# Attention on one NeuronCore: the value projection with its operands swapped, and the logits' scale, bias and row extreme in one VectorE instruction per block

## The chip, the cores and the metric

The kernel runs on one NeuronCore of a Trainium2 chip. The metric is the device time of one execution in microseconds (us); the time of a kernel is the median of its runs. Engines: PE is TensorE, DVE is VectorE, ACT is ScalarE, POOL is GpSimd, SP issues the weight transfers.

## What is computed

256 tokens of width 1024 go through three layers in float32. Layer A has a convolution and pooling mixer, layers B and C an attention mixer; each mixer is followed by a feed-forward block with a causal convolution, and layer C also by a gate of a side input. The two attention mixers are what the change touches:

```
q, k, v = split(rmsnorm(h) @ w_in)            # 16 heads of 64 each (layer C: 4 of the values are 128 wide)
# layer B: 8 "moba" heads (causal softmax with a table bias), 8 "fox" heads (forgetting bias)
p = softmax(q @ k.T * 64**-0.5 + bias, causal);  y = p @ v
# layer C: 4 "diff" heads: y = (softmax(q1 k1 + b1) - lam * softmax(q2 k2 + b2)) @ v, then an RMS norm
#          8 "stick" heads: stick-breaking weights from log_sigmoid and a suffix sum, y = w @ v
h = h + y @ w_out
```

## The kernel before

**Projections.** Activations lie with channels on partitions and tokens along the free dimension. Every float32 weight block is split into a rounded high part `wh` (ACT, line 480) and the rest `wl` (DVE, line 785, or POOL, line 434). A unit (`unit`) is 24 matmuls: 8 blocks of 128 input channels, three products each (lines 1243 to 1245), weights stationary, 256 tokens moving. Weights stream through a ring of four slots; the split of unit u+4 begins when unit u is done. A norm's factor `rstd` is applied after the projection: the reader of the bank multiplies by `rstd`.

**Attention.** `attention` exists once for each engine. The work is in 8 pairs of heads, 3 units each: q is unit 3n, k is 3n+1, v is 3n+2. Layer 0 of `attention` (layer B of the model) has four moba and four fox pairs, layer 1 four diff and four stick pairs. The order on each engine is written out by hand in a loop over j. For pair n, PE runs `scores(n)` (lines 1354 and 1356 for moba, fox and diff), and after two or three units `turn(n)`: it transposes the values (line 1377) and the softmax's result (line 1392), and `weigh(n)` multiplies the two (lines 1415 and 1417). Between `scores` and `turn` stand DVE's `logits(n)` (scale and bias: lines 1038 and 1040; row maxima: lines 1043 and 1045), ACT's `softmax_exp(n)` (line 641: four exponentials with their sums) and DVE's `normalise(n)` (lines 1059 and 1065). DVE's `read_out(u)` (line 1019) copies each unit of q, k or v out of its bank, times `rstd`. ACT's `copy_turned` takes the transposes out of PSUM: line 657 the probabilities, line 659 the values.

**Banks.** The units use three banks in turn, unit 3 of each layer a fourth. A unit waits on the semaphore `bank_read` until the unit three before it has been read. The first two units of an attention stage are begun by `begin`, behind the last unit of a down projection, whose two banks are read by `residual_down` (line 950, two counts of `bank_read` for each chunk).

Of the kernel before, what the change touches and what calls it, by code (L numbers as in the profile page):

```python
# [75 lines left out]
def build_program(nc, streams, x_in, p_in, vectors_in, pool_in, gate_in, rel_in, onehot_in, count_in, out):  # L76
# [55 lines left out]
    with ExitStack() as ctx:  # L132
# [37 lines left out]
        lam = sb("lam", [P, 8])  # L170
        eps = sb("eps", [P, 1])
# [50 lines left out]

        stick_values = psum[:, 5, SEQ:2 * SEQ].rearrange("p (b d) -> p b d", b=2)
# [3 lines left out]
        EARLY = QKV_BANKS  # L227

        def qkv_bank(u):
            return turned_banks[:, 0, 0:SEQ] if u == EARLY else psum[:, u % QKV_BANKS, 0:SEQ]  # L230

# [69 lines left out]
        turned_read = sem("turned_read")  # L301
        relu_done = sem("relu_done")
# [170 lines left out]
        def _(act):  # L473
# [149 lines left out]
            def attention(layer, name, out_name):  # L623
# [10 lines left out]
                def softmax_exp(n):  # L634
# [3 lines left out]
                    for half in range(2):  # L638
                        for b, (a, z) in enumerate(((0, P), (P, SPAN))):
                            at = 2 * b + half  # L640
                            last = nc.scalar.activation(e[:, half, a:z], e[:, half, a:z], ACT.Exp,  # L641
# [4 lines left out]
                def copy_turned(n):  # L646
# [8 lines left out]
                    else:  # L655
                        m = 1 if order[n][0] == "diff" else 2
                        nc.scalar.activation(probs_t[n % 2][:, 0:m, :], turned_banks[:, 0:m, 0:SPAN], ACT.Copy)
# [33 lines left out]
                for j in range(PAIRS + 2):  # L691
# [9 lines left out]
                    if j < PAIRS:  # L701
                        round_next(3 * j)
                    if late:
                        log1p(j - 1)
# [73 lines left out]
        def _(dve):  # L778
# [32 lines left out]
            def norm_scale(n):  # L811
# [7 lines left out]
                steps(nc.vector.reciprocal(rstd[:, :], root))  # L819
# [40 lines left out]
            def small_work():  # L860
# [8 lines left out]
                nc.vector.tensor_copy(table, aux[0:ROWS, 2, :]).then_inc(table_ready, 1)  # L869
# [142 lines left out]
            def attention(layer, name, out_name):  # L1012
# [3 lines left out]
                def read_out(u):  # L1016

                    dve.wait_ge(units_done, base[name] * RING + u + 1)
                    nc.vector.tensor_tensor(qkv[:, u, :], qkv_bank(u), rstd[:, :], ALU.mult).then_inc(bank_read, 1)  # L1019
# [4 lines left out]
                def logits(n):  # L1024
# [9 lines left out]
                    if kind == "fox":  # L1034
                        b = bias[:, HEADS:HEADS + 1, :].to_broadcast([P, 2, SEQ])
                    else:
                        b = bias[:, 2 * (c - 4):2 * (c - 4) + 2, :]
                    first = steps.mark(nc.vector.scalar_tensor_tensor(e[:, :, 0:P], S[:, :, 0:P], HD ** -0.5, b[:, :, P:SEQ],
                                                                      ALU.mult, ALU.add))
# [626 lines left out]
```

## Time and profile before

| | |
|---|---|
| median of 3 runs | 968.26 us (967.33 to 969.67) |
| profiled execution, own time | 968.35 us |
| its span | 966.6 us |
| mean granted TensorE clock | 0.987 |
| busy: PE, DVE, ACT, POOL | 934.3, 649.6, 526.6, 314.7 us |
| attention of layer 0 | from 286.7 us to about 400 us |
| attention of layer 1 | from 603.9 us to about 720 us |

The profiled execution took 968.35 us, 1.75 us more than its span. Busy shares are means over stages; the idle time in front of an instruction, with the one that ended it, tells where an engine waited.

### The profile page before, as it was taken

Reading aid. Unit: us, or ns where it says so; the run is one execution under the profiler, and the core shown is the slowest. Engines: PE = TensorE matmul, PEld = TensorE weight load, DVE = VectorE, ACT = ScalarE, POOL = GpSimd, SP = SyncE. Lnnn points to the kernel's source line nnn. Section 1 sums busy time; section 2 is a strip of 40 time slices with the busy share of each in tenths; the row PEclk is TensorE's granted clock in tenths of the full one; section 3 lists DMA queues with packets and bytes.
Section 4 is the critical chain, followed back from the end, with each engine's and each line's share of the span. In section 5 each row is a group of like instructions: output and inputs, shape, how many; then the busy total and the mean of one; then the engine's idle time right before and its main releaser. Section 6 shows DMA issues by size and latency. Waiting matters only on the chain.

```text
span 966.6 us, 20895 instructions
## 1 busy us (share of the span) xinstructions
PE 934.3 (97%) x7618; PEld 910.7 (94%) x7618; DVE 649.6 (67%) x1133; ACT 526.6 (54%) x847; POOL 314.7 (33%) x134
## 2 busy tenths in 40 slices
PE   8899999999998999999999999999999999999993
PEld 7789999999997999999999999989999999999993
DVE  6998676665456776676666555797557877765376
ACT  6345665555444555575555544556557766654443
POOL 3343343444410001334443441000224434444552
PEclk9899999999999999999999999999999999999997
DMA  7535865567542533375556754344335655665421
GB/s 245 184 110 196 229 221 192 183 201 251 183 146 87 171 135 119 123 234 186 186 175 195 233 182 135 125 155 141 107 106 180 194 187 185 188 218 192 159 81 45
DMA packets 46329, 163.52 MB, mean 169 GB/s; under 512 B 5010, under 2 KB 9746, under 8 KB 46277
## 3 DMA queue, kind: packets, MB, share of 16 engines
q1 hardware_dynamic: 41704, 158.19, 49.6%
q10 hardware_dynamic: 4573, 4.62, 1.8%
q8 instruction: 34, 0.56, 0.2%
q14 instruction: 18, 0.15, 0.0%
HBM read 161.71 MB, written 3.44 MB: 171 GB/s over the span
## 4 chain that ended last, share of the span: by engine, by line
PE 80%; DVE 8%; issue 6%; ACT 3%; POOL 1%; DMA 1%; SPq 0%; DVEq 0%; POOLq 0%; ACTq 0%
PE psum L1243 25%; PE psum L1244 24%; PE psum L1245 24%; POOL wl L434 1%; DVE h L1218 1%; PE psum L1415 1%; DMA raw<-in_even_in 1%; DVE wl L785 1%; ACT wh L480 1%; DVE work L882 1%; PE psum L1392 1%; DVE xs L801 1%; PE psum L1384 1%; PE psum L1356 1%; ACT xs L502 0%
## 5 line engine op out<-in xcount | busy, mean ns | idle before, releaser
L434 POOL TENSOR_TENSOR wl<-raw,wh 128x1024 fp32r<-128x1024 f32 (+2 forms) x113 | 297.3, 2631 | 614.9 <-ACT wh L480 614.8
L1243 PE MATMUL psum<-xs,wh 128*128 128x256 f32 x1632 | 467.8, 287 | 6.9 <-DVE wl L785 4.2
L1244 PE MATMUL psum<-xs,wh 128*128 128x256 f32 x1632 | 462.9, 284 | 0.0
L1245 PE MATMUL psum<-xs,wl 128*128 128x256 f32 x1632 | 462.8, 284 | 0.0
L480 ACT ACTIVATE wh<-raw 128x1024 fp32r<-128x1024 f32 (+2 forms) x270 | 301.2, 1119 | 264.6 <-PE psum L1245 252.8
L1243 PEld LDWEIGHTS psum<-xs,wh 128*128 128x128 f32 x1632 | 314.4, 193 | 13.7 <-DVE wl L785 5.4
L1244 PEld LDWEIGHTS psum<-xs,wh 128*128 128x128 f32 x1632 | 314.4, 193 | 0.2
L1245 PEld LDWEIGHTS psum<-xs,wl 128*128 128x128 f32 x1632 | 314.3, 193 | 0.0
L785 DVE TENSOR_TENSOR wl<-raw,wh 128x1024 fp32r<-128x1024 f32 (+1 forms) x157 | 203.9, 1301 | 99.4 <-ACT wh L480 99.0
L1243 PE MATMUL psum<-ys,wh 128*128 128x256 f32 x672 | 191.8, 285 | 0.0
L1244 PE MATMUL psum<-ys,wh 128*128 128x256 f32 x672 | 190.7, 284 | 0.0
L1245 PE MATMUL psum<-ys,wl 128*128 128x256 f32 x672 | 190.7, 284 | 0.0
L1243 PEld LDWEIGHTS psum<-ys,wh 128*128 128x128 f32 x672 | 129.6, 193 | 0.8 <-issue 0.7
L1244 PEld LDWEIGHTS psum<-ys,wh 128*128 128x128 f32 x672 | 129.6, 193 | 0.1
L1245 PEld LDWEIGHTS psum<-ys,wl 128*128 128x128 f32 x672 | 129.5, 193 | 0.0
L833 DVE SCALAR_TENSOR_TENSOR psum<-work,vec,psum 128x256 f32<-128x256 f32 x176 | 85.3, 485 | 56.1 <-ACT psum L591 53.0
L801 DVE SCALAR_TENSOR_TENSOR xs<-h,vec,xs 128x256 fp32r<-128x256 f32 (+1 forms) x56 | 61.0, 1098 | 29.1 <-ACT xs L502 28.7
L824 DVE TENSOR_TENSOR work<-psum,rstd 128x256 f32<-128x256 f32 x112 | 47.1, 421 | 19.8 <-PE psum L1245 19.1
L591 ACT ACTIVATE psum<-work,vec 128x256 f32<-128x256 f32 x88 | 49.4, 561 | 9.7 <-DVE work L824 9.4
L502 ACT ACTIVATE xs<-h,vec 128x256 fp32r<-128x256 f32 (+1 forms) x48 | 24.3, 506 | 40.4 <-DVE h L928 26.5
L641 ACT ACTIVATE work<-work,row_max 128x128 f32<-128x128 f32 (+1 forms) x48 | 21.3, 444 | 34.5 <-DVE row_max L1045 25.8
L1019 DVE TENSOR_TENSOR qkv<-psum,rstd 128x256 f32<-128x256 f32 x48 | 19.7, 418 | 15.7 <-PE psum L1245 15.7
(195 smaller groups left out, 708.6 us busy)
## 6 DMA issues: line engine op xcount, KB each, us to landing
raw<-in_up SPq DMA_DIRECT2D x132, 512.0 KB, 3.8
raw<-in_down SPq DMA_DIRECT2D x48, 704.0 KB, 4.3
raw<-in_qkv SPq DMA_DIRECT2D x48, 512.0 KB, 3.3
raw<-in_even_in SPq DMA_DIRECT2D x16, 512.0 KB, 4.2
raw<-in_out SPq DMA_DIRECT2D x16, 512.0 KB, 3.2
raw<-in_ple SPq DMA_DIRECT2D x8, 640.0 KB, 3.9
raw<-in_even_out SPq DMA_DIRECT2D x8, 512.0 KB, 3.3
toeplitz_dram<-table_dram ACTq DMA_DIRECT2D x1, 2048.0 KB
```

What stands on the lines that cost most here:

```text
L434: nc.gpsimd.tensor_tensor(low, raw[:, s, 0:tiles * P], high.bitcast(f32), ALU.subtract)\
L480: nc.scalar.activation(split_weights(q, s, tiles * P)[0], raw[:, s, 0:tiles * P], ACT.Copy).then_inc(hi_ready, 1)
L502: nc.scalar.activation(xs[:, ds(m, 1), 0, :], h[:, ds(m, 1), :], ACT.Identity, scale=column(VECTORS[n][0], m)).then_inc(xh_ready, 1)
L591: nc.scalar.activation(target, padded[:, 2:2 + SEQ], ACT.Identity, bias=column(bias_name, chunk), scale=column(taps, chunk + 2 * chunks)). ...
L641: last = nc.scalar.activation(e[:, half, a:z], e[:, half, a:z], ACT.Exp, bias=row_max[:, n % 2, at:at + 1], accum_out=row_sum[:, n % 2, at ...
L785: nc.vector.tensor_tensor(low, raw[:, s, 0:tiles * P], high.bitcast(f32), ALU.subtract).then_inc(lo_ready[s], 1)
L801: nc.vector.scalar_tensor_tensor(xs[:, ds(m, 1), 1, :], h[:, ds(m, 1), :], column(VECTORS[n][0], m), xs[:, ds(m, 1), 0, :].bitcast(f32), A ...
L824: return nc.vector.tensor_tensor(out_ap, proj[:, s, 0:SEQ], rstd[:, :], ALU.mult)
L833: return nc.vector.scalar_tensor_tensor(out_ap, padded[:, k:k + SEQ], column(taps, chunk + k * chunks), out_ap, ALU.mult, ALU.add)
L1243: nc.tensor.matmul(bank, high_w[:, w], high, start=first, stop=False)
L1244: nc.tensor.matmul(bank, high_w[:, w], low, start=False, stop=False)
L1245: done = nc.tensor.matmul(bank, low_w[:, w], high, start=False, stop=last)
```

## The change

- Values: the v blocks of two neighbouring pairs are projected together by units 6g+2 and 6g+3. In them `xs` (128 tokens) is stationary and 256 weight columns move, so the result has tokens on partitions and needs no transpose. Each of the two units holds four of the eight channel blocks of both pairs; both add into one bank, 512 columns wide. The host lays out the weights accordingly (`projection_units`). There are still 24 units of 24 matmuls for each layer.
- ACT's `read_values(g)` copies them out, with `token_rstd` as a scale for each partition: two instructions for two pairs. `turn_rstd` (PE, two matmuls of one column) and `read_token_rstd` (DVE) make `token_rstd` once a layer.
- `turn` has no value transposes, `copy_turned` no value copy, and DVE has 16 read-outs a layer instead of 24.
- Since pair n+1 with n even has its q and k in units 3n+4 and 3n+5, `scores` of odd pairs stands behind the next unit.
- The logits: negated, scaled, biased and with their row minimum in one `tensor_tensor_reduce` for each head and block, four in place of two and two; the table is scaled by 8 and `softmax_exp` uses scale -1.
- The bank a unit takes and what it waits for are new (`bank_use`, `bank_free`), and the wait of the first two units of a stage, too.

```diff
+        def is_value(u):
+            return u % 6 in (2, 3)
+        def bank_use(u):
+            return 5 * (u // 6) + (0, 1, 2, 2, 3, 4)[u % 6]
+        def scores_behind(kind, n):
+            return n % 2 == 1 or kind == "stick"
...
-                    source = stick_values if order[n][0] == "stick" else turned_banks[:, :, SPAN:SPAN + P]
-                    nc.scalar.activation(qkv[:, 3 * n + 2, :].rearrange("p (b d) -> p b d", b=2), source, ACT.Copy)\
-                      .then_inc(turned_read, 1)
+                def read_values(g):
+                    u = 6 * g + 3
+                    act.wait_ge(units_done, base[name] * RING + u + 1)
+                    act.wait_ge(token_ready, layer + 1)
+                    for b in range(2):
+                        last = nc.scalar.activation(qkv[:, u - 1:u + 3:3, b * P:(b + 1) * P],
+                                                    qkv_bank(u)[:, b * SEQ:(b + 1) * SEQ].rearrange("p (c d) -> p c d", c=2),
+                                                    ACT.Identity, scale=token_rstd[:, b:b + 1])
+                    last.then_inc(values_read, 1)
...
-                    first = steps.mark(nc.vector.scalar_tensor_tensor(e[:, :, 0:P], S[:, :, 0:P], HD ** -0.5, b[:, :, P:SEQ],
-                                                                      ALU.mult, ALU.add))
-                    second = steps.mark(nc.vector.scalar_tensor_tensor(e[:, :, P:SPAN], S[:, :, P:SPAN], HD ** -0.5, b,
-                                                                       ALU.mult, ALU.add))
-                    steps.wait(first)
-                    nc.vector.tensor_reduce(row_max[:, n % 2, 0:2], e[:, :, 0:P], AX.X, ALU.max, negate=True)
-                    steps.wait(second)
-                    last = nc.vector.tensor_reduce(row_max[:, n % 2, 2:4], e[:, :, P:SPAN], AX.X, ALU.max, negate=True)
+                    for half in range(2):
+                        b = bias[:, HEADS if kind == "fox" else 2 * (c - 4) + half, :]
+                        for block, (a, z, first) in enumerate(((0, P, P), (P, SPAN, 0))):
+                            at = 2 * block + half
+                            last = nc.vector.tensor_tensor_reduce(e[:, half, a:z], S[:, half, a:z], b[:, first:SEQ], -HD ** -0.5,
+                                                                  -NEG, ALU.add, ALU.min, row_max[:, n % 2, at:at + 1])
...
+                def value_unit(u):
+                    s, bank, first = u % RING, qkv_bank(u), u % 6 == 2
+                    pe.wait_ge(lo_ready[s], q0 + u // RING + 1)
+                    for i in range(DC // 2):
+                        t, w = i + (0 if first else DC // 2), slice(i * SEQ, (i + 1) * SEQ)
+                        for b in range(2):
+                            tokens, sums = slice(b * P, (b + 1) * P), bank[:, b * SEQ:(b + 1) * SEQ]
+                            nc.tensor.matmul(sums, xs[:, t, 0, tokens], wh[:, s, w], start=first and i == 0 and b == 0, stop=False,
+                                             skip_group_check=True)
+                            nc.tensor.matmul(sums, xs[:, t, 0, tokens], wl[:, s, w], start=False, stop=False, skip_group_check=True)
+                            last = nc.tensor.matmul(sums, xs[:, t, 1, tokens], wh[:, s, w], start=False,
+                                                    stop=not first and i == DC // 2 - 1, skip_group_check=True)
+                    last.then_inc(units_done, 1)
...
-                    pe.wait_ge(bank_read, q0 * RING + max(3 * n + 3, EARLY + 1))
-                    if n >= 1:
-                        pe.wait_ge(turned_read, N)
-                    for b in range(2):
-                        target = stick_values[:, b, :] if order[n][0] == "stick" else turned_banks[:, b, SPAN:SPAN + P]
-                        nc.tensor.transpose(target, qkv[:, 3 * n + 2, b * P:(b + 1) * P], ident[:, :])
...
-                begin(q0, (0, 1), qkv_bank, lambda s: q0 * RING + s - QKV_BANKS + 1, from_xs,
+                begin(q0, (0, 1), qkv_bank, lambda s: q0 * RING, from_xs,
                       lambda t: pe.wait_ge(xl_ready, DC * n_norm + t + 1))
```

The first place is DVE's queue in layer 0 before the first pair's probabilities are ready. Before: the split of unit 6's weights, the logits of pair 0, unit 3's read-out, the first of `normalise`.

```order
L785 TENSOR_TENSOR wl<-raw,wh 128x1024 [waits hi_ready]
L1038 SCALAR_TENSOR_TENSOR work<-psum,bias 128x2x128 [waits bias_landed,s_done]
L1040 SCALAR_TENSOR_TENSOR work<-psum,bias 128x2x256
L1043 TENSOR_REDUCE row_max<-work 128x2 [waits dve_step]
L1045 TENSOR_REDUCE row_max<-work 128x2 [waits dve_step]
L1019 TENSOR_TENSOR qkv<-psum,rstd 128x256 [waits units_done]
L1059 RECIPROCAL row_inv<-row_sum 128x4 [waits exp_done]
```

Of the change, the same place:

```order
L814 TENSOR_TENSOR wl<-raw,wh 128x1024 [waits hi_ready]
L1078 ISA work,row_max<-psum,bias 128x128 [waits bias_landed,s_done]
L1078 ISA row_max 128x1
L1078 ISA work,row_max<-psum,bias 128x256
L1078 ISA row_max 128x1
L1078 ISA work,row_max<-psum,bias 128x128
L1078 ISA row_max 128x1
L1078 ISA work,row_max<-psum,bias 128x256
L1078 ISA row_max 128x1
L1058 COPY token_rstd<-psum 128x2 [waits token_turned]
L1093 RECIPROCAL row_inv<-row_sum 128x4 [waits exp_done]
```

Four instructions have become eight: each reduce is followed by a row that writes its one column. The read-out has gone, a small copy has come.

The second place is PE's queue in layer 0 from the end of unit 5 to the start of unit 6. Before:

```order
L1245 MATMUL psum<-xs,wl 128x256
L1377 MATMUL psum<-ident,qkv 128x128 [waits bank_read]
L1377 MATMUL psum<-ident,qkv 128x128
L1392 MATMUL psum<-ident,work 128x128 [waits norm_done]
L1392 MATMUL psum<-ident,work 128x128 x5
L1354 MATMUL psum<-qkv 128x128 [waits logits_done,bank_read]
L1354 MATMUL psum<-qkv 128x128
L1356 MATMUL psum<-qkv 128x256 x2
L1243 MATMUL psum<-xs,wh 128x256 [waits bank_read,lo_ready2]
```

Of the change:

```order
L1282 MATMUL psum<-xs,wl 128x256
L1462 MATMUL psum<-ident,work 128x128 [waits token_ready,norm_done]
L1462 MATMUL psum<-ident,work 128x128 x5
L1280 MATMUL psum<-xs,wh 128x256 [waits lo_ready2,values_read]
L1281 MATMUL psum<-xs,wh 128x256
```

The two value transposes are gone, `scores(1)` (which read lines 1354 and 1356 before) stands behind unit 6, and unit 6 waits for ACT's `read_values`.

## Rows read from the trace of the kernel before

**Rows 1.** Busy time by engine, a feed-forward stretch: engines, PEclk, DMA share, GB/s

```profile
460.00:480.00 20.00, 20.00 (x169) 20.00 (x169) 12.69 (x24) 10.78 (x17) 8.03 (x4) 1.00 0.55 167
```

**Rows 2.** PE in order of time, layer 0, one whole pair: start, us, instruction

```profile
324.59 0.38 PE L1377 MATMUL psum<-ident,qkv 128*128 128x128 f32 x2
324.81 0.82 PE L1392 MATMUL psum<-ident,work 128*128 128x128 f32 x6
325.56 0.49 PE L1354 MATMUL psum<-qkv 64*128 64x128 f32 x4
...
336.13 0.38 PE L1377 MATMUL psum<-ident,qkv 128*128 128x128 f32 x2
```

**Rows 3.** PE in order of time, layer 0, the first pair and unit 6

```profile
308.91 0.44 PE L1377 MATMUL psum<-ident,qkv 128*128 128x128 f32 x2
311.73 0.88 PE L1392 MATMUL psum<-ident,work 128*128 128x128 f32 x6 [2.38 <-DVE work L1065]
...
313.68 0.58 PE L1243 MATMUL psum<-xs,wh 128*128 128x256 f32 x1
...
316.40 0.31 PE L1243 MATMUL psum<-xs,wh 128*128 128x256 f32 x1
```

**Rows 4.** PE's busy time and granted clock in stretches of 1 us

```profile
71.00:72.00 1.00, 1.00 (x6) 0.50 0.00 0
313.00:314.00 1.00, 1.00 (x7) 0.52 0.00 0
```

**Rows 5.** PE in order of time, two other waits

```profile
70.46 1.04 PE L1517 MATMUL psum<-work,qkv 128*128 128x256 f32 x2 [2.21 <-DVE work L891]
...
415.51 0.38 PE L1243 MATMUL psum<-xs,wh 128*128 128x256 f32 x1 [1.35 <-DVE xs L801]
```

**Rows 6.** DVE in order of time, layer 0, the first pair

```profile
306.59 0.41 DVE L1038 SCALAR_TENSOR_TENSOR work<-psum,bias 128x256 f32<-128x256 f32 x1
306.92 0.68 DVE L1040 SCALAR_TENSOR_TENSOR work<-psum,bias 128x512 f32<-128x512 f32 x1
307.52 0.41 DVE L1043 TENSOR_REDUCE row_max<-work 128x2 f32<-128x256 f32 x1
307.85 0.68 DVE L1045 TENSOR_REDUCE row_max<-work 128x2 f32<-128x512 f32 x1
308.44 0.41 DVE L1019 TENSOR_TENSOR qkv<-psum,rstd 128x256 f32<-128x256 f32 x1
310.45 0.18 DVE L1059 RECIPROCAL row_inv<-row_sum 128x4 f32<-128x4 f32 x1 [1.60 <-ACT work L641]
310.66 1.01 DVE L1065 TENSOR_SCALAR work<-work,row_inv 128x128 f32<-128x128 f32 x4
```

**Rows 7.** ACT in order of time, layer 0, the first pair

```profile
308.86 0.19 ACT L641 ACTIVATION_READ_ACCUMULATOR work<-work,row_max 128x1 f32 x1
308.95 0.49 ACT L641 ACTIVATE work<-work,row_max 128x256 f32<-128x256 f32 x1
...
313.85 0.36 ACT L659 ACTIVATE qkv<-psum 128x256 f32<-128x256 f32 x1
```

**Rows 8.** PE in order of time, the start of layer 0's attention

```profile
286.57 0.28 PE L1245 MATMUL psum<-ys,wl 128*128 128x256 f32 x1
286.69 0.28 PE L1243 MATMUL psum<-xs,wh 128*128 128x256 f32 x1
```

**Rows 9.** DVE in order of time, the same place

```profile
286.96 0.42 DVE L950 TENSOR_TENSOR h<-h,psum 128x256 f32<-128x256 f32 x1 [0.92 <-PE psum L1245]
```

**Rows 10.** PE in order of time, layer 1, waits of the first three pairs

```profile
624.21 0.55 PE L1392 MATMUL psum<-ident,work 128*128 128x128 f32 x3 [0.72 <-DVE work L1076]
...
635.30 0.70 PE L1422 MATMUL psum<-diff,ones 128*128 128x256 f32 x2 [0.22 <-ACT diff L671]
...
637.23 0.49 PE L1354 MATMUL psum<-qkv 64*128 64x128 f32 x4 [0.69 <-DVE qkv L1019]
...
641.81 0.45 PE L1415 MATMUL psum<-work,qkv 128*128 128x256 f32 x1 [0.59 <-ACT qkv L659]
```

More of the change, by code:

```diff
@@ L170, in build_program @@
         lam = sb("lam", [P, 8])
+        token_rstd = sb("token_rstd", [P, 2])
         eps = sb("eps", [P, 1])
@@ L640, in softmax_exp @@
                             at = 2 * b + half
-                            last = nc.scalar.activation(e[:, half, a:z], e[:, half, a:z], ACT.Exp,
+                            last = nc.scalar.activation(e[:, half, a:z], e[:, half, a:z], ACT.Exp, scale=-1.0,
                                                         bias=row_max[:, n % 2, at:at + 1],
@@ L702, in attention @@
                         round_next(3 * j)
+                    if j < PAIRS and j % 2 == 1:
+                        read_values(j // 2)
                     if late:
@@ L1131, in attention @@
                     late = turn and order[j - 1][0] == "stick"
-                    if turn and not late:
+                    behind = turn and scores_behind(order[j - 1][0], j - 1)
+                    if turn and not behind:
                         logits(j - 1)
-                    if j < PAIRS:
+                    if j < PAIRS and not is_value(3 * j):
                         read_out(3 * j)
+                    if behind and not late:
+                        logits(j - 1)
+                    if j == 1:
+                        read_token_rstd()
                     if is_diff(j - 3):
@@ L1320, in values, with turn_rstd @@
+                def turn_rstd():
+                    pe.wait_ge(rstd_ready, n_norm + 1)
+                    for b in range(2):
+                        last = nc.tensor.matmul(token_bank[:, b:b + 1], rstd[:, b * P:(b + 1) * P], ident[:, 0:1], start=b == 0, stop=True,
+                                                skip_group_check=True)
+                    last.then_inc(token_turned, 1)
                 def values(n, b, a, z):
@@ L1431, in attention @@
                 for j in range(1, PAIRS):
-                    late = order[j - 1][0] == "stick"
+                    behind = scores_behind(order[j - 1][0], j - 1)
                     if j == 1:
-                        qkv_unit(EARLY)
-                    if not late:
+                        qkv_unit(3)
+                    if not behind:
                         scores(j - 1)
-                    if j > 1:
+                    if j == 1:
+                        turn_rstd()
+                    else:
                         qkv_unit(3 * j)
-                    if late:
+                    if behind:
                         scores(j - 1)
@@ L1579, in weight_units, with projection_units @@
     return np.ascontiguousarray(tiles.reshape(m, P, split, k // split, P).transpose(0, 2, 1, 3, 4)).reshape(m * split, P, -1)
+def projection_units(w, pairs):
+    plain = weight_units(w, range(w.shape[1] // P))
+    rows = w.reshape(2, DC // 2, P, w.shape[1] // P, P)
+    units = []
+    for a, b in zip(pairs[0::2], pairs[1::2]):
+        values = rows[:, :, :, [a[2], b[2]], :].transpose(0, 2, 1, 3, 4).reshape(2, P, -1)
+        units += [plain[a[0]], plain[a[1]], values[0], values[1], plain[b[0]], plain[b[1]]]
+    return np.ascontiguousarray(np.stack(units))
 def channel_columns(v):
```

65 lines of the change are left out of this document (45 added, 20 removed).

## The prediction

> **What bounds the kernel now.** I read the busy time by stage first, then the order of time on PE with the waits in it, and then the queues of DVE and ACT where PE waits. In a feed-forward stretch PE has no gap: 169 matmuls in 20 us, 118 ns each, while DVE is busy for 12.69 us and ACT for 10.78 us [rows 1]. PE's queue sets the time there, and the change leaves it alone. In attention, a settled pair of layer 0 also runs without a gap on PE: 11.54 us from one pair's value transposes to the next's [rows 2]. The reader should see three exceptions, all at the start of a layer's attention. The first pair of layer 0 keeps PE waiting 2.38 us for `normalise` [rows 3], and behind it the granted clock reads 0.52, half of the full level, so the lower of the two, 1.2 GHz [rows 4]. In layer 1 PE waits 0.72, 0.22, 0.69 and 0.59 us in the first three pairs [rows 10], each time for DVE, or for ACT that stands behind DVE. Elsewhere a shorter queue of DVE or ACT is worth nothing.
>
> **Part 1, value transposes, a gain.** In a settled pair they take 324.81 - 324.59 = 0.22 us of PE [rows 2]. There are 8 pairs in each of two layers. Seven in layer 0 are on PE's path: 7 x 0.22 = 1.54 us. The first pair's lie inside PE's wait and give nothing by themselves. In layer 1 I count five (pairs 2 to 6), 1.10 us: the first two pairs are set by DVE, below, and in the last pair PE waits for the stick chain, which starts from `scores` and does not get shorter; I take 0.2 us back for that.
>
> **Part 2, the value units.** Each is 24 matmuls, each with a 128x128 weight load and 256 moving columns, as before. The row for such a pair of load and matmul is 118 ns [rows 1], whichever operand is x. I take 0 for the difference. From both sides: a first matmul after another kind of work costs up to 0.1 us more, over 16 units 0 to +1.6 us; nothing in the rows speaks for a gain.
>
> **Part 3, the logits.** Now 306.59 to 308.44, 1.85 us [rows 6]. The starts give the rate: 256 elements 0.33 us (306.59 to 306.92), 512 elements 0.60 us, so 0.27 us for 256 elements and 0.06 us fixed. Four new instructions of 128, 256, 128 and 256 elements take 2 x (0.20 + 0.33) = 1.06 us. Each is followed by an instruction that writes the extreme. The trace has no such row on DVE. ACT's counterpart occupies 308.95 - 308.86 = 0.09 us [rows 7]; the smallest DVE operation shown takes 0.18 us [rows 6]; the bounds are 0 and 0.30 us (a 128-element instruction with a dependent wait). I take 0.13 us, between the two nearest rows: 1.06 + 4 x 0.13 = 1.6 us, so 0.25 us less than now for each logits. The Trainium skill, VectorE: DVE Perf Modes, section Two Vector instructions with no wait between them, says that an operation which also writes out its accumulator is two instructions, the main one and an accumulator read. No DVE row here shows it; with the read counted at nothing the sum below would be 1.6 us better.
>
> Where is it on the path? In the first pair of layer 0, and in the first two of layer 1. In layer 0 the DVE queue ahead of `normalise(0)` loses unit 2's read-out (0.33 us) and 0.25 us of logits: 0.6 us. ACT's exponentials do not change. `normalise` ends its wait at about 311.1 in place of 311.7. The new two small matmuls for `token_rstd` (some 0.35 us of PE) and DVE's small copy (0.17 us, while ACT computes) lie in that wait; without it they would cost 0.35 us.
>
> **Part 4, the clock.** Twelve matmuls from 313.68 to 316.40 take 2.72 us [rows 3]; at 118 ns they would take 1.4. So the low clock costs 1.3 us. It fell after waits of 2.38 us [rows 3] and 2.21 us [rows 5, 4], and after one of 1.35 us PE went on without a slow row [rows 5]. The new wait: PE starts its unit 5 later by the 0.35 us of the small matmuls and has no value transposes in it, `normalise` is 0.6 us earlier, so it is about 1.8 us, midway between kept and lost. I take kept, by a hair: gain 1.3 us.
>
> **Part 5, layer 1's first pairs.** DVE is the queue that PE waits for. It loses the read-outs of units 2 and 3 (0.67 us) and 0.25 us in each of the first two logits, but `scores(1)` now stands behind unit 6. `turn(0)` comes 0.3 us sooner, half of what DVE saves, since its split of unit 6's weights then waits for ACT; `scores(2)`, which needs unit 7's read-out, itself behind `normalise(1)` and a split, 0.2 us sooner; `weigh(1)` at 641.81 waited for ACT's value copy of 0.36 us [rows 7, 10], which is gone from there, so 0.8 us sooner in all. With the 1.10 and -0.2 us of part 1: 1.7 us.
>
> **Part 6, the start of both stages, a loss.** The first unit of the stage starts at 286.69, one matmul pitch behind the last of the down projection [rows 8]. It waits for `bank_read` two short of the stage's count, which is the read of the bank that it takes; the other bank's read is DVE's addition from 286.96 to 287.38 [rows 9]. With the new wait (the full count, for both units) PE may not start before that addition has ended: 287.38 + 0.06 - 286.69 = 0.75 us, and 0.1 us for a first matmul after a wait. Everything behind it (the statistics, `rstd`, the chain to `normalise`) starts from PE, so nothing takes it back: 0.85 us a layer, 1.7 us in all. Bounds: 0.7 to 0.9 us a layer. What is queued behind the waiting matmul is the whole stage.
>
> **Part 7, order and banks, counted at nothing.** `scores` of an odd pair stands one unit (24 x 0.118, 2.8 us) later. To `turn` there are left two units, 5.7 us, and `weigh`: a pair's 11.54 us less three units and 0.97 us of transposes leave 2.1 us for `scores` and `weigh`, about half each, so 6.7 us [rows 1, 2]. The chain is logits 1.6, exponentials 1.9 (308.53 to 310.45), `normalise` 1.2 us (310.45 to 311.67) [rows 6], in all 4.7 and some tenths for handing over: covered by about 1.5 us. Unit 7's read-out, needed by the next `scores`, has about 0.3 us left. The next unit's wait for `read_values` (two ACT instructions of 0.36 to 0.49 us [rows 7], behind one rounding of weights) ends about when `turn` does. If the cover goes, each of the three odd pairs of a layer costs what is missing.
>
> **The sum.** Layer 0: 0.6 + 1.3 + 1.54 = 3.4 us. Layer 1: 1.7 us. Start of stages: -1.7 us. Together 3.4 us less. Against the profiled execution's 968.35 us, which is the median of the runs within 0.1 us, that is 964.9 us. POOL and the weight transfers of SP are as before.
>
> **Rivals.**
> 1. *The clock falls all the same* (the wait of 1.8 us is nearer to 2.21 than I think): 1.3 us less gain, 966.2 us. For it: 2.21 us was enough; against: 1.35 was not.
> 2. *The extreme is nearly free* (read-outs of 0.05 us): three logits on the path, 0.3 us each, 964.0 us with the clock kept.
> 3. *The new instruction runs at half rate, and DVE becomes the bound.* Then 128 and 256 elements cost 0.33 and 0.60 us, logits 2 x 0.93 + 4 x 0.13 = 2.4 us, 0.8 us more than taken. Three of them on the path cost 2.4 us; unit 7's read-out and its like in the odd pairs come late by 0.8 - 0.3 = 0.5 us, three times in layer 0 (1.5 us), some in layer 1 (0.5 us); the first wait grows to 2.6 us and the clock falls (1.3 us). 964.9 + 5.7 = 970.6 us, slower than before. It decides from logits of about 2.0 us on. For it: none of the rows is such an instruction. Against: the reduce and the two-source operation each run at one element per cycle, 0.27 us for 256 elements [rows 6]. The Trainium skill, Vector Engine (DVE) Microarchitecture Reference, section Points that are easy to get wrong, warns that a scalar-tensor-tensor form with two non-bf16 SBUF sources halves throughput, as no port is left for the accumulator; here one source is PSUM, and no run here shows which side that falls on.
> 4. *The change loses its gain at the start of the stages and in the odd pairs* (logits of 1.7 to 2.0 us and a lost clock): 967 to 968.5 us, no difference.
>
> **Numbers.** Within 0.2% is within 1.9 us of 968.3, about what a measurement of this kernel can tell. Chances: the forecast 0.38, rival 1 0.26 (faster, just), rival 2 0.08, rival 3 0.10, rival 4 0.18. The range goes from 963.0 (free extreme, cheap start) to 969.0, which leaves out rival 3 and little else. The likeliest case's own range is 963.8 to 966. Faster by over 0.2%: 0.67, within it 0.23, slower 0.10.
>
> **What would show it.** PE idle for about 0.8 us in front of the first `xs` matmul of each attention stage, by DVE's residual addition (part 6). No transposes of `qkv`; pairs in layer 0 of 11.3 us (part 1). Logits of 1.6 us from first start to the end of the fourth read (part 3). A wait of about 1.8 us in front of `turn(0)`, and a clock of 1.00 or 0.5 in the 4 us behind it (part 4). New waits of PE for unit 7's, 13's or 19's read-out would make part 7 wrong, value units of more than 2.9 us part 2.

## The result, and the profile after

The changed kernel takes 961.05 us (median of 4 runs, 959.69 to 961.81) against 967.83 us of the kernel before beside it (4 runs). The ratio is 0.9936, with a 95% interval from 0.9919 to 0.9953: faster by 0.5 to 0.8%. I had forecast 964.9 us, and a range from 963.0 to 969.0 us. The sign was right, but the time lies below the range, and the gain was 6.8 us where I had worked out 3.4. So the question is not whether the parts work, but which of them were priced wrongly.

From the page of the profile after (its span is 6.7 us shorter, and PE's share stays at 97%):

```profile
span 959.9 us, 20891 instructions
PE 929.6 (97%) x7594; PEld 907.3 (95%) x7594; DVE 634.3 (66%) x1167; ACT 527.8 (55%) x847; POOL 314.2 (33%) x134
```

PE in order of time (start, us, instruction, and in brackets the wait with its releaser), at the start of layer 0's attention, its first four pairs, the first matmul of the up projection behind it, and the first pairs of layer 1:

```profile
286.08 0.28 PE L1282 MATMUL psum<-ys,wl 128*128 128x256 f32 x1
287.14 0.35 PE L1280 MATMUL psum<-xs,wh 128*128 128x256 f32 x1 [0.78 <-DVE h L980]
...
311.18 0.87 PE L1462 MATMUL psum<-ident,work 128*128 128x128 f32 x6 [1.43 <-DVE work L1099]
...
322.35 0.82 PE L1462 MATMUL psum<-ident,work 128*128 128x128 f32 x6
323.10 0.49 PE L1426 MATMUL psum<-qkv 64*128 64x128 f32 x4
...
333.67 0.82 PE L1462 MATMUL psum<-ident,work 128*128 128x128 f32 x6
...
344.80 0.82 PE L1462 MATMUL psum<-ident,work 128*128 128x128 f32 x6
...
410.94 0.38 PE L1280 MATMUL psum<-xs,wh 128*128 128x256 f32 x1 [1.01 <-DVE xs L830]
...
619.84 0.49 PE L1462 MATMUL psum<-ident,work 128*128 128x128 f32 x3
...
632.33 0.49 PE L1426 MATMUL psum<-qkv 64*128 64x128 f32 x4 [0.91 <-DVE qkv L1054]
...
636.26 0.67 PE L1487 MATMUL psum<-work,qkv 128*128 128x256 f32 x2
```

Four readings. PE now stands in front of the stage's first unit for DVE's residual addition: part 6 of the prediction. The wait in front of the first pair's turning (the transposes of its probabilities) is 1.43 us for 2.38 [rows 3]. The pairs take 333.67 - 322.35 = 11.32 us and then 344.80 - 333.67 = 11.13 us, in turn, where before each took 11.54 us [rows 2]: the 0.22 us of the value transposes, and in every other pair 0.2 us that I had not counted. In layer 1 one wait is left of the four in [rows 10], the one in front of `scores(2)`, and it has grown from 0.69 to 0.91 us; a new one of 0.18 us stands in front of the last pair.

DVE in order of time: the addition at the stage's start, and the first pair's logits:

```profile
286.47 0.42 DVE L980 TENSOR_TENSOR h<-h,psum 128x256 f32<-128x256 f32 x1 [0.92 <-PE psum L1282]
...
306.77 0.28 DVE L1078 CUSTOM_DVE_ANT_0 work<-psum,bias 128x128 f32<-128x128 f32 x1
306.98 0.09 DVE L1078 DVE_READ_ACCUMULATOR2_ANT row_max<- 128x1 f32 x1
306.98 0.42 DVE L1078 CUSTOM_DVE_ANT_0 work<-psum,bias 128x256 f32<-128x256 f32 x1
307.32 0.08 DVE L1078 DVE_READ_ACCUMULATOR2_ANT row_max<- 128x1 f32 x1
...
307.88 0.16 DVE L1058 COPY token_rstd<-psum 128x2 f32<-128x2 f32 x1
309.90 0.18 DVE L1093 RECIPROCAL row_inv<-row_sum 128x4 f32<-128x4 f32 x1 [1.86 <-ACT work L659]
```

This is the view that decides part 3. The read of the extreme is there, 0.09 us long, but the next fused instruction has the same start, 306.98. The main instructions follow one another by 0.21 us (128 elements) and 0.34 us (256), so the logits take 307.88 - 306.77 = 1.11 us, for the 1.85 us of [rows 6], and for the 1.6 us that I had forecast.

PE's busy time and granted clock in the microsecond of [rows 4]:

```profile
313.00:314.00 1.00, 1.00 (x10) 1.00 (x10) 1.00 (x3) 1.00 (x2) 0.00 (x0) 1.00 0.38 78
```

The granted clock (the number behind POOL's 0.00) is 1.00 where it was 0.52: the upper of the two levels, 2.4 GHz.

**The stages.** The change acts in the two attention stages alone. I measure a stage from one matmul pitch (0.12 us) behind the start of the last `ys` matmul of the down projection to the first matmul of the up projection: layer 0 from 286.20 to 410.94 us, 124.74 us, for 286.69 to 415.51 us, 128.82 us, before [rows 5, 8]. Layer 1 goes from 603.93 to 731.85 us, 127.92 us, before, and from 599.36 to 725.15 us, 125.79 us, after. So 4.08 us came off layer 0 and 2.13 us off layer 1, 6.2 us in all. The stretch between the stages (188.42 us) and the one behind them (234.75 us) are the same in both kernels. The stretch ahead, from the first projection matmul to layer 0's attention, was 274.9 to 277.7 us long in the 14 profiled executions of this study, whatever the kernel. So most of the scatter of whole times, the clock apart, lies ahead of the attention, and the experiments below are read by their stages first. For two executions of a kernel a stage agreed within 0.1 us, but for the clock (below). Against that, most medians of the table that follows differ by less than their intervals are wide.

### The profile page after: what moved, and what is told of

The parts are those of the page before. It is cut to its first block, busy times and chain, and to the rows that moved or that the text cites. A ratio compares the mean times of both kernels' runs of the same rounds, so it can differ in the third digit from the quotient of the medians.

```text
span 959.9 us, 20891 instructions
## 1 busy us (share of the span) xinstructions
PE 929.6 (97%) x7594; PEld 907.3 (95%) x7594; DVE 634.3 (66%) x1167; ACT 527.8 (55%) x847; POOL 314.2 (33%) x134
## 4 chain that ended last, share of the span: by engine, by line
PE 77%; DVE 9%; issue 7%; ACT 4%; POOL 1%; DMA 1%; SPq 0%; DVEq 0%; POOLq 0%; ACTq 0%
PE psum L1280 23%; PE psum L1281 23%; PE psum L1282 23%; DVE wl L814 2%; POOL wl L452 1%; PE psum L1377 1%; DVE h L1255 1%; PE psum L1379 1%; PE psum L1380 1%; ACT wh L498 1%; PE psum L1487 1%; DMA raw<-in_even_in 1%; DVE work L912 1%; PE psum L1462 1%; DVE xs L830 1%
## 5 line engine op out<-in xcount | busy, mean ns | idle before, releaser
L1280 PE MATMUL psum<-xs,wh 128*128 128x256 f32 x1504 | 429.9, 286 | 7.1 <-DVE wl L814 2.0
L1281 PE MATMUL psum<-xs,wh 128*128 128x256 f32 x1504 | 426.1, 283 | 0.0
L1282 PE MATMUL psum<-xs,wl 128*128 128x256 f32 x1504 | 426.0, 283 | 0.0
L1280 PEld LDWEIGHTS psum<-xs,wh 128*128 128x128 f32 x1504 | 289.2, 192 | 10.7 <-issue 5.0
L1281 PEld LDWEIGHTS psum<-xs,wh 128*128 128x128 f32 x1504 | 289.2, 192 | 0.1
L1282 PEld LDWEIGHTS psum<-xs,wl 128*128 128x128 f32 x1504 | 289.1, 192 | 0.0
L1377 PE MATMUL psum<-wh,xs 128*128 128x256 f32 x128 | 37.1, 290 | 0.0
```

Source lines behind the costliest of these rows:

```text
L1280: nc.tensor.matmul(bank, high_w[:, w], high, start=first, stop=False)
L1281: nc.tensor.matmul(bank, high_w[:, w], low, start=False, stop=False)
L1282: done = nc.tensor.matmul(bank, low_w[:, w], high, start=False, stop=last)
L1377: nc.tensor.matmul(sums, xs[:, t, 0, tokens], wh[:, s, w], start=first and i == 0 and b == 0, stop=False, skip_group_check=True)
```

## The experiments

| kernel | layer 0, us | layer 1, us | median, us | ratio to before, 95% |
|---|---|---|---|---|
| before | 128.82 | 127.92 | 967.83 | |
| changed | 124.74 | 125.79 | 961.05 | 0.9936 (0.9919 to 0.9953) |
| e1, old start | 123.74 | 124.92 | 958.84 | 0.9915 (0.9897 to 0.9932) |
| e2, all scores behind | 124.35 | 125.78 | 959.58 | 0.9935 (0.9915 to 0.9956) |
| e3, order alone | 128.22 | 128.82 | 966.60 | 0.9997 (0.9985 to 1.001) |
| e4, logits alone | 127.79; 126.24 | 126.45; 126.46 | 962.94 | 0.9957 (0.9941 to 0.9973) |
| e5, old logits | 125.64; 127.14 | 127.47; 127.52 | 964.35 | 0.9975 (0.9964 to 0.9986) |
| e6, e1 and e2 | 123.31 | 124.91 | 959.41 | 0.9921 (0.9907 to 0.9934) |
| e7, longer wait | 127.79 | 125.79 | 962.23 | 0.9947 (0.9933 to 0.9962) |
| e8, slower logits | 127.37; 125.81 | 125.79; 125.80 | 963.72 | 0.9962 (0.9949 to 0.9974) |
| e9, e6 and gate sums later | 121.53 | 124.95 | 956.39 | 0.9896 (0.9874 to 0.9918) |

Two numbers are two profiled executions of the same kernel, whose whole times were 966.05 and 963.06 us (e4), 963.09 and 964.03 (e5), 962.75 and 961.64 (e8). The kernel before, run beside these, had medians of 966.14 (e1, e2, e4, e5), 966.93 (e3, e6, e7, e8) and 966.47 us (e9).

**e1, the condition at the start of a stage.**

```diff
-                begin(q0, (0, 1), qkv_bank, lambda s: q0 * RING, from_xs,
+                begin(q0, (0, 1), qkv_bank, lambda s: q0 * RING + s - QKV_BANKS + 1, from_xs,
```

> The changed kernel, with the matmuls of an attention stage's first two units waiting for as few bank reads as before the change (each for its own bank). Theory A (this wait costs its whole length, as part 6 had it): the waits of 0.78 and 0.63 us at the start of the two stages go, and the time falls by 1.4 to 1.7 us against the changed kernel, to about 959.5 us. Rival: the first unit's later tiles wait for the normalised activations instead, which come at a pace of their own, so that the loss is made good within the unit: less than 0.5 us. The trace decides by the wait of the first matmul and by the time from it to the first value unit.

PE in order of time at the start of layer 0's attention:

```profile
284.99 0.28 PE L1282 MATMUL psum<-ys,wl 128*128 128x256 f32 x1
285.11 0.28 PE L1280 MATMUL psum<-xs,wh 128*128 128x256 f32 x1
```

The first `xs` matmul follows the last `ys` matmul by 0.12 us, for 1.06 us in the changed kernel. The stages are 1.00 and 0.87 us shorter, and every later period is the same. The loss was real, and nothing took it back; it was 1.9 us where part 6 had 1.7, and where the expectation had 1.4 to 1.7.

**e2, the scores of every pair behind the next pair's first unit.**

```diff
-            return n % 2 == 1 or kind == "stick"
+            return True
```

> The changed kernel, with the scores of every pair behind the next pair's first unit, not only those of odd pairs (on TensorE and on VectorE). Theory A (a change between kinds of matmul costs PE some 0.2 us, and scores that stand beside the weighing save one): the even settled pairs become as short as the odd ones, 11.1 us for 11.3 and 11.6 for 11.8, which is three pairs of layer 0 and one of layer 1: 0.8 us less, about 960.2 us. Rival (the odd pairs are shorter because less of their work is in them, or by where their units' banks lie, and not by the order): the pairs keep their alternating lengths, 961.0 us. Second rival: the later scores leave too little work ahead of the turning, which waits again: slower than 961.5 us with a wait at the turning in each even pair.

PE in order of time, layer 0, the pair that took 11.32 us in the changed kernel:

```profile
320.22 0.82 PE L1462 MATMUL psum<-ident,work 128*128 128x128 f32 x6
...
323.84 0.49 PE L1426 MATMUL psum<-qkv 64*128 64x128 f32 x4
...
324.69 0.65 PE L1487 MATMUL psum<-work,qkv 128*64 128x256 f32 x4
...
331.34 0.82 PE L1462 MATMUL psum<-ident,work 128*128 128x128 f32 x6
```

The pair takes 331.34 - 320.22 = 11.12 us; so do its like (11.13, 11.58, 11.58, 11.57 us, no longer alternating), 0.2 us less in three pairs. But the period up to the last pair's turning went from 8.05 to 8.25 us, so that the stage gained 0.39 us, and layer 1 nothing: there the wait of 0.91 us in front of `scores(2)` only became one of 1.12 us in front of `weigh(1)`, which comes 36.89 us after the stage's start for 36.90. What holds `weigh(1)` back no experiment shows. Theory A holds for the pairs' lengths, and its total was too high; that the cost belongs to any change between kinds of matmul is more than the rows bear out (part 7 below).

**e3, the kernel before with the new order alone.** On PE and on DVE the scores and logits of odd pairs stand behind the next pair's first unit:

```diff
-                    late = order[j - 1][0] == "stick"
+                    late = order[j - 1][0] == "stick" or (j - 1) % 2 == 1
```

> The kernel before, with nothing of the change but the order: the scores and logits of odd pairs stand behind the next pair's first unit, as in the changed kernel. Theory A (a change between kinds of matmul costs PE 0.2 us wherever it stands, and scores directly ahead of the weighing save one): every settled pair with odd number is 0.2 us shorter, 11.34 us for 11.54 and 11.8 for 12.0, three in layer 0 and two in layer 1: about 1.0 us less over the two stages. Rival (the shorter odd pairs belong to the values' new form, where the order costs or gives nothing): both stages as long as before, within 0.2 us. Second rival (with logits of 1.85 us the later scores are not turned in time): waits at the turning, a longer time than before.

PE in order of time: three pairs of layer 0, and two waits in layer 1:

```profile
334.67 0.38 PE L1380 MATMUL psum<-ident,qkv 128*128 128x128 f32 x2
...
346.01 0.38 PE L1380 MATMUL psum<-ident,qkv 128*128 128x128 f32 x2
...
357.99 0.38 PE L1380 MATMUL psum<-ident,qkv 128*128 128x128 f32 x2
...
633.79 0.70 PE L1425 MATMUL psum<-diff,ones 128*128 128x256 f32 x2 [0.54 <-ACT diff L671]
...
663.92 0.67 PE L1418 MATMUL psum<-work,qkv 128*128 128x256 f32 x2 [0.37 <-ACT qkv L659]
```

The odd pair takes 11.34 us for 11.54, the even one behind it the old 11.98. Layer 0 is shorter by 0.60 us, three times 0.2: the order gives this by itself, without the values' new form. In layer 1 the same order costs 0.90 us, with logits of 1.85 us. It is lost in two places: 0.34 us where the wait of 0.22 us in [rows 10] has become 0.54, and 0.56 us around the new wait of 0.37 us. Neither wait is in the changed kernel, where the logits are shorter. So theory A holds in layer 0; in layer 1 the second rival holds, with waits in front of other matmuls than the turning. The whole is no different from before.

**e4, the kernel before with the new logits alone.**

```diff
-                    first = steps.mark(nc.vector.scalar_tensor_tensor(e[:, :, 0:P], S[:, :, 0:P], HD ** -0.5, b[:, :, P:SEQ],
...
+                            last = nc.vector.tensor_tensor_reduce(e[:, half, a:z], S[:, half, a:z], b[:, first:SEQ], -HD ** -0.5,
+                                                                  -NEG, ALU.add, ALU.min, row_max[:, n % 2, at:at + 1])
```

> The kernel before, with only the new logits (one fused instruction for each block, the table scaled, the sign turned in the exponential). Theory A (a block's extreme comes free of time on VectorE's queue): the logits take 1.11 us for 1.85, which is on the path three times (2.2 us), and the first wait of layer 0 gets shorter than 1.8 us so that the clock stays at 1.0 (1.3 us): 3.5 us less than before, 964.3 us. Theory B (the read of the extreme costs 0.13 us each, as part 3 had it, and the rest of the gain lies elsewhere): 1.6 us for the logits, 2.1 us less than before, 965.7 us.

The table's scale and the exponential's sign go with it, as in the change. Layer 1 is 1.47 us shorter: 0.74 us for each of the two logits on the path, where I had 0.25. In layer 0 the first turning comes 0.75 us sooner after the stage's start (24.29 us for 25.04). The stage itself came out at 127.79 us and, the second time, at 126.24 us. The clock makes the difference. PE in order of time, the first execution:

```profile
311.15 1.39 PE L1387 MATMUL psum<-ident,work 128*128 128x128 f32 x6 [1.94 <-DVE work L1060]
```

and the second:

```profile
309.75 0.88 PE L1387 MATMUL psum<-ident,work 128*128 128x128 f32 x6 [1.95 <-DVE work L1060]
```

The waits are equal, and the six transposes take 1.39 us the one time and 0.88 us the other. The whole time can't settle it by itself: the median, 962.94 us, is 3.2 us below the 966.14 of the kernel before beside it, between the 2.5 and 4.0 us that the stages of the two executions gained, and nearer to theory A (3.5) than to B (2.1). The 1.85 us of the logits are 1.11 here too, as theory A has it; that the clock would stay up, which it also had, came true in one execution of two.

> A second profiled execution of the logits-only kernel (first turning waits 1.94 us, after which the granted clock was 0.5 for 3 us). Theory A (same program, same clock): again 0.5 there, 127.8 us for the stage. Theory B (differs between executions): the clock may stay at 1.0, and the stage is 126.3 us.

**e5, the changed kernel with the old logits** (the edit of e4 the other way round).

> The changed kernel, with the old logits (two additions over both heads, then two reductions), so that only the value path and the order are of the change. Theory A: the logits are 0.74 us longer at three places on the path, 2.2 us more than the changed kernel; the first wait of layer 0 grows from 1.43 us to about 2.2 us and, should the clock fall after it as it did in the kernel before, 1.3 us more: 963.2 to 964.5 us. Theory B (most of the time came off by the values and the order): no more than 1.2 us above the changed kernel, 962.2 us or less.

DVE in order of time, the first pair:

```profile
305.31 0.41 DVE L1077 SCALAR_TENSOR_TENSOR work<-psum,bias 128x256 f32<-128x256 f32 x1
305.65 0.68 DVE L1079 SCALAR_TENSOR_TENSOR work<-psum,bias 128x512 f32<-128x512 f32 x1
306.25 0.41 DVE L1082 TENSOR_REDUCE row_max<-work 128x2 f32<-128x256 f32 x1
306.57 0.67 DVE L1084 TENSOR_REDUCE row_max<-work 128x2 f32<-128x512 f32 x1
307.17 0.15 DVE L1058 COPY token_rstd<-psum 128x2 f32<-128x2 f32 x1
```

The logits are back at 307.17 - 305.31 = 1.86 us. PE's first wait is 2.17 us for 1.43, which is the same 0.74 us. Layer 0 is 0.90 us longer and layer 1 1.68 us, so the fused instruction is worth 2.6 us by this way of taking it apart, and 0.75 + 1.47 = 2.2 us by e4. Theory B, which had at most 1.2 us for it, is out.

> A second profiled execution of the values-only kernel (old logits; first turning waits 2.17 us, after which the granted clock stayed at 1.0). Theory A (the same program gets the same clock in this place): again no stretch at 0.5 in layer 0, 125.6 us for the stage. Theory B (whether the clock falls after a wait of about 2 us differs from one execution to the next): it may be at 0.5 for 3 us, and the stage 127.1 us.

Again the two executions differ: 125.64 us with the clock at 1.00, 127.14 us with it at 0.50 from 311 to 312 us.

**e7, a longer wait, and e8, slower logits in all pairs of layer 0.** A memset on DVE, which only takes time (0.36 us), stands ahead of the logits, in e7 four times and for n == 0 only, in e8 two times and for every pair:

```diff
+                    if layer == 0:
+                        for _ in range(2):
+                            steps(nc.vector.memset(mid_rstd[:, :], 0.0))
```

> The changed kernel with four small instructions that only take time (each fills an unused tile of layer 0, and waits for the one before) ahead of the logits of layer 0's first pair: the first turning waits about 2.6 us for 1.43. Theory A (part 4: the length of PE's wait decides on its clock): the granted clock falls to 0.5 for some 3 us behind it, as in the kernel before, and the stage is 1.2 + 1.3 to 1.5 us longer. Theory B (it is decided by where the wait lies and what PE did around it, since the logits-only kernel fell after 1.94 us and the values-only kernel did not after 2.17 us): the clock may stay at 1.0, and the stage is 1.2 us longer.

> The changed kernel with two of these small instructions (about 0.6 us together) ahead of the logits of every pair of layer 0. Theory A (VectorE is on the path only in the first pair; part 3): stage 0 grows by those 0.6 us once, and the settled pairs keep 11.1 to 11.8 us. Rival (VectorE's shorter work is what shortens the settled pairs): each of the seven other pairs is longer too, 2 us or more in all.

> A second profiled execution of the kernel with slower logits in layer 0 (first turning waits 2.22 us, after which the granted clock was lower). Theory A (same program, same clock): the low stretch is there again, 127.4 us for the stage. Theory B (differs between executions): the clock may stay at 1.0, and the stage is 125.9 us.

PE in order of time and in stretches of 1 us (granted clock behind the bracket) for e7:

```profile
311.46 0.88 PE L1465 MATMUL psum<-ident,work 128*128 128x128 f32 x6 [3.00 <-DVE work L1102]
```

```profile
312.00:313.00 1.00, 1.00 (x9) 0.69 0.00 0
313.00:314.00 1.00, 1.00 (x7) 0.50 0.00 0
```

for the first execution of e8:

```profile
310.23 1.52 PE L1465 MATMUL psum<-ident,work 128*128 128x128 f32 x6 [2.22 <-DVE work L1102]
```

and for the second:

```profile
310.83 0.87 PE L1465 MATMUL psum<-ident,work 128*128 128x128 f32 x6 [2.22 <-DVE work L1102]
```

The wait of e7 is 1.57 us longer than in the changed kernel, and the stage 3.05 us longer: 1.5 us are the clock's. That is as theory A says, but theory B allowed it too. e8 tells the two apart: the same program, the same wait of 2.22 us, and once the lower level, once not. With e4 (1.94 and 1.95 us) and e5 (2.17 and 2.16 us) it is one of two in each of three programs. The clock stayed up in all four kernels with a wait of 1.43 to 1.54 us and fell in all three executions with 2.38 us (before, e3) or 3.00 us (e7). So theory A as I wrote it (the wait's length decides) is wrong for waits of about 2 us: executions of one program differ there, and the price is 1.50 to 1.56 us each time. A second place in every trace says the same, PE's wait in layer A that is the first of [rows 5]. No experiment touched it, and the clock fell behind it in nine executions with 2.20 to 2.22 us and in two with 1.88 us; it stayed up with 1.76, with 1.79 and, in the first execution of e8, with 2.22 us:

```profile
68.42 0.70 PE L1594 MATMUL psum<-work,qkv 128*128 128x256 f32 x2 [2.22 <-DVE work L921]
```

The Trainium skill, TensorE: Matmul & The Clock Gate, section Part 1: The HAM clock gate, says that the gate looks at PE's activity in windows that run freely and don't start with the kernel. That would make two executions differ, and the pairs agree with it; no run here shows the windows themselves.

On its other question, e8's layer 0 took 125.81 us in the execution at full clock, 1.07 us more than the changed kernel: 0.79 us in the first wait, and 0.3 us in the last pairs (11.88 us for 11.78, 8.24 us for 8.05). The five pairs between kept their times. VectorE's shorter queue is worth nothing in a settled pair.

**e6, e1 and e2 together.**

> The changed kernel with both edits of the first runs: the old condition at the start of a stage, and the scores of all pairs behind the next pair's first unit. By the trace of the two edits alone (1.00 and 0.87 us for the start, 0.39 and 0.01 us for the order) the stages should take 123.3 and 124.9 us if the two are independent, 2.3 us less than in the changed kernel, 958.7 us. Rival: the earlier start only moves the first pair's wait, which then grows as the scores come later; less than 1.5 us off the changed kernel.

123.31 and 124.91 us: to within 0.05 us what the two edits gave alone, so they are independent. The median, 959.41 us, is 0.7 us above what was expected, and its ratio lies within the interval of e1; the 0.4 us between them can't be told by whole runs here.

**e9, e6 with the sums of the forget gates behind the first logits.**

```diff
+                    if layer == 0 and j == 1:
+                        forget_sums()
...
-                    if layer == 0 and j == 0:
-                        forget_sums()
...
+                    qkv_unit(3 * j + 2)
                     if layer == 0 and j == 1:
                         pe.wait_ge(f_sums, 1)
...
-                    qkv_unit(3 * j + 2)
```

> The kernel with both edits (old condition at the start, all scores behind the next unit), in which VectorE's sums of the forget gates (six small instructions, about 2.6 us) stand behind the logits of layer 0's first pair instead of ahead of them, and TensorE turns them behind unit 5 instead of ahead of it. Theory A (the first turning waits because of what stands ahead of the first logits on VectorE): the logits start 2.6 us sooner, the wait of 1.54 us goes, and stage 0 takes 121.8 to 122.0 us for 123.31; the whole about 957.5 us. Rival: the sums then come too late for TensorE's turning of them or for the normalising, and a new wait of 1 us or more takes the place of the old.

DVE in order of time, the first pair:

```profile
301.98 0.27 DVE L1078 CUSTOM_DVE_ANT_0 work<-psum,bias 128x128 f32<-128x128 f32 x1
...
303.16 0.40 DVE L1147 SCALAR_TENSOR_TENSOR work<-work 8x256 f32<-8x256 f32 x1
...
305.80 0.18 DVE L1093 RECIPROCAL row_inv<-row_sum 128x4 f32<-128x4 f32 x1
306.02 1.01 DVE L1099 TENSOR_SCALAR work<-work,row_inv 128x128 f32<-128x128 f32 x4
```

PE in order of time, the same place:

```profile
307.03 0.28 PE L1522 MATMUL psum<-ident,fcum 8*128 8x8 f32 x2
307.24 0.87 PE L1462 MATMUL psum<-ident,work 128*128 128x128 f32 x6
```

The turning has no wait left, and theory A holds. The stage is 121.53 us, 1.78 us less than in e6, where the wait was 1.54 us; the rest comes off the stretch from the end of `scores(0)` to the end of the turning, where the turning of the gate's sums no longer stands between the two units (7.04 us without the wait in e6, 6.78 us here). The gate's sums now run while ACT computes the exponentials, where DVE stands idle for 1.86 us in the changed kernel. This is the fastest version: 956.39 us, against 961.05 us of the change, though in another session; by the ratios to the kernel before, 0.9896 for 0.9936, with intervals that just don't meet. With e6 (0.9907 to 0.9934) its interval overlaps, and there the stage alone shows the gain.

## Why the prediction was right in its sign and wrong in its size

**Part 1, value transposes: right.** The even pairs of layer 0 went from 11.54 to 11.32 us, by 0.22 us.

**Part 2, value units: right.** An old unit and a value unit, one behind the other, take 5.85 us (from 316.50 to 322.35), as two old units did before (318.74 to 324.59).

**Part 3, logits: this is the step that failed.** The term "I take 0.13 us, between the two nearest rows", for the read of the extreme behind each fused instruction, was mis-sized: the read's row of 0.08 to 0.09 us lies beside the instruction that follows, and the starts show no time of the queue for it. The low bound, 0, was the truth. I had 0.25 us less for each logits; it is 0.74 us. That it is on the path three times was right (e4, e5), so the term was worth 2.2 to 2.6 us for 0.75. Why did I leave the bound? I took ACT's row for the nearest, where the read occupies 0.09 us of the queue [rows 7]. The rule of the Trainium skill that I quoted (VectorE: DVE Perf Modes, section Two Vector instructions with no wait between them) is borne out: two instructions. The sentence that priced the second at nothing, 1.6 us less, was the better sum. Rival 3, half rate, is excluded: 256 elements take 0.34 us, start to start, for the 0.33 us of [rows 6]. The read-out that left DVE's queue ahead of the first normalising gave what was forecast: in e1, which has the old start, the first turning comes 1.08 us sooner after the stage's start (23.96 us for 25.04), and 0.34 us of it are not the logits'.

**Part 4, the clock: right in the outcome, and partly by luck.** It was kept, and worth 1.5 us for 1.3; the twelve matmuls that I counted left out the scores of pair 1 ahead of them, which took 1.15 us for 0.86. But the wait was 1.43 us and not 1.8 us, and it was shorter because of the error of part 3: with the old logits it was 2.17 us (e5), and 0.25 us off them would have left 1.9 us. There the outcome would have been open: the clock fell in one of two executions at 1.94 us, and in layer A twice at 1.88 us and not at 1.79 or 1.76 us.

**Part 5, layer 1: mis-sized, by the same term.** `turn(0)` has no wait. `weigh(1)` comes 36.90 us after the stage's start for 37.88 us, and with the start's 0.87 us taken out 1.85 us sooner, where I had 0.8. Two logits at 0.5 us more than forecast are the difference. Behind `weigh(1)` the stage gained 1.15 us, 0.17 of it in front of the up projection, where part 1 had 0.9 for the transposes: that part was right here, too.

**Part 6, the start: right.** 1.00 and 0.87 us for 0.85 each (e1).

**Part 7, order "counted at nothing": the second step that failed.** It looked only for what the order could cost. e3 shows that it gives 0.60 us in layer 0. The rows show where. PE in order of time, one pair of the kernel before (its turning starts at 324.81 [rows 2]) and then its last pair:

```profile
326.42 0.39 PE L1243 MATMUL psum<-xs,wh 128*128 128x256 f32 x1
...
329.48 0.65 PE L1415 MATMUL psum<-work,qkv 128*64 128x256 f32 x4
...
392.22 0.82 PE L1392 MATMUL psum<-ident,work 128*128 128x128 f32 x6
392.79 0.36 PE L1243 MATMUL psum<-ys,wh 128*128 128x256 f32 x1
```

and an odd pair of the changed kernel, whose turning starts at 333.67:

```profile
334.24 0.36 PE L1280 MATMUL psum<-xs,wh 128*128 128x256 f32 x1
...
337.28 0.49 PE L1426 MATMUL psum<-qkv 64*128 64x128 f32 x4
...
338.14 0.65 PE L1487 MATMUL psum<-work,qkv 128*64 128x256 f32 x4
```

Six transposes occupy PE for 0.57 us when a projection unit follows (333.67 to 334.24, and 392.22 to 392.79 before), and for 325.56 - 324.81 = 0.75 us when the scores follow [rows 2]. The value transposes apart, nothing else in the pair differs by more than 0.02 us: the scores take 0.86 us in either place (325.56 to 326.42; 337.28 to 338.14), and the unit between takes 3.06 us before and 3.04 us after. So the cost isn't one of every change between kinds of matmul, of which a pair has five in either order. It lies in the transposes directly in front of the scores, and the new order takes the scores away from there at no price elsewhere. What PE does in these 0.2 us no run here shows.

**What is left.** PE's wait in front of the up projection went from 1.35 to 1.01 us in layer 0 [rows 5] and from 1.15 to 0.98 us in layer 1, 0.5 us together. In layer 0 either the new logits (e4) or the new values (e5) alone are enough for it, and the order alone is not (e3, 1.36 us). In layer 1 the new values do it (e5, 0.99 us), and the new logits alone do not (e4, 1.15 us). Why it shrank is open: I made no run for it.

So the 6.2 us of the stages against 3.4 forecast: about 1.6 us more from the logits, 0.6 from the order, 0.5 in front of the up projections, 0.2 from the clock, and 0.2 less from the start. That sums to 2.7 of the 2.8 us. The forecast counted from 968.35 us, and the kernel before took 967.83 us beside the change; the rest of the 6.8 us lies ahead of the stages, where executions differ anyway.

The range was wrong for the same reasons. Its low end, 963.0 us, held the free extreme at 1.6 us less, but no gain from the order and none in front of the up projections.

## What to carry to other kernels

An edit that reorders PE's work can gain as well as cost: read from the trace how long the same group of matmuls occupies PE with either follower, since here one neighbour cost 0.2 us and the others nothing more. When an operation issues a second instruction, look at the start of the next one and not at the second's duration, and don't take another engine's row for it. A bound that three places on the path depend on is a case of its own in the forecast, with its full price. Where a wait of PE of about 2 us decides on the clock, keep two cases, here 1.5 us apart; better, move what stands ahead of the chain, as e9 does, and the question is gone.

## What the runs showed of the hardware that I had not expected

- The accumulator read behind a fused DVE instruction has a row of 0.07 to 0.09 us, and the next fused instruction has the same start: four of them for 768 elements took 1.11 us.
- The granted clock after PE waits of 1.94 to 2.22 us was 1.0 in one execution and 0.5 in the other of the same program, in three programs out of three; the lower level cost 1.50 to 1.56 us. In layer A a wait of 2.20 to 2.22 us was followed by the lower level in nine executions of ten.
- Six transposes followed by matmuls over 64 rows (the scores) took 0.75 us, and 0.57 us followed by a projection over 128; the scores took 0.86 us wherever they stood.
